# Seven block products in place of eight for a SwiGLU up-projection

## The chip, the cores and the metric

One Trainium2 chip, one of its cores. The metric is the device time of one execution of the whole program in microseconds (us), median of several runs.

## The reference

One decoder layer, sequence 1024, width 1024, all in float32: three token mixers behind one input projection, an output projection, then the feed-forward part, which is what changes here:

```python
def swiglu(h, w_up, w_down):
    gate, val = jnp.split(h @ w_up, 2, axis=-1)
    return (jax.nn.silu(gate) * val) @ w_down
...
        h = rmsnorm(x, norm_ffn[l]) * (1.0 + sc_ffn) + sh_ffn
        x = x + gt_ffn * swiglu(h, w_ffn_up[l], w_ffn_down[l])
    return rmsnorm(x, norm_final)
```

`w_up` is 1024 x 5632 (2816 gate columns, 2816 value columns), `w_down` 2816 x 1024.

## The kernel before

Every float32 matrix is kept as a high part (rounded to the type that TensorE takes, `F32R`) and a low part (the rest), and a product is three matmuls, the `PASSES`: high by high, high by low, low by high. The mixers take the first 1865 us. The change leaves them alone but for a pair of semaphores at the start; what follows is the feed-forward part, `ffn_sp`, `ffn_pool`, `ffn_pe`, `ffn_act` and `ffn_dve`, one function for each engine's queue. The order of the work on an engine is the order in which it is written there; semaphores alone tie the engines together.

The normed activations stand in `h_hi` and `h_lo`, channels on partitions: 8 blocks of 128 channels by 1024 tokens. The loop has 11 steps (`F_STEPS`) of 256 feed-forward columns. In a step TensorE makes eight up-projection units in `UP` (banks 0 to 3), each a column block of 128 by one half of the tokens: 24 matmuls of 512 columns (L180, 8 channel blocks by 3 passes), gate and value in turn. ScalarE takes exp(-gate) from the bank (L2207). VectorE adds 1, takes the reciprocal, multiplies by gate and by value (L2237 to L2241), ScalarE rounds the result to `hid_hi` (L2209), VectorE subtracts for `hid_lo` (L2243). Then TensorE makes 16 down-projection units in `DOWN` (banks 4 to 7), 6 matmuls each (L2191), and VectorE adds each to the residual rows `x1`, in `feat_region` (L2248). The hidden part of a step thus hides behind its later up units, and the 16 adds behind the down units.

SyncE loads raw weights in halves of 512 KB to `w_raw`. GpSimd splits them into high (L161, a cast) and low (L163, a subtraction), into `A_W` for a step's first column block and `B_W` for its second; for `w_down` it first multiplies by the adaLN gates (L2149), then splits to `D_W` (L2150, L2152). GpSimd waits for `up` or `down` before it writes over a buffer. At the end each 128 tokens are normed and stored as their adds are done (`final_norm`).

`D_W` begins at this byte:

```python
    D_W = [over(f"wD_{h}", [P, 2, D], F32R, at_byte["rows_region"] + (4104 + n * 2048) * 4)
           for n, h in enumerate(("hi", "lo"))]
```

In the built program `rows_region`, `h_hi`, `h_lo` and `A_W` begin at multiples of 64 bytes, so `D_W` begins 32 bytes past one; so does `O2_W`, the last weights of the output projection (L1002).

Of the kernel before, what the change touches and what calls it, by code (L numbers as in the profile page):

```python
# [76 lines left out]
def _build(ctx, nc, x, c, ada_w, ada_b, norm_mix, norm_ffn, w_in, gla_w_g2, gla_b_g2, gla_norm,  # L77
# [2045 lines left out]
    def ffn_pool(pool, step):  # L2123
        own = Count(sem("w_split"))
        wait_unit(pool, unit_of("out", NT - 1, 2))
        for j in range(2):
            pool.wait_ge(sem(f"w_in{j}"), 16 * (IN_ALL + 1))
            split(pool, j, A_W, P, own)
        for g in range(GROUPS):
            i, n = divmod(g, 3)  # L2130
            if n == 0:
                if i:
                    pool.wait_ge(sem("up"), 8 * i)
                else:
                    wait_unit(pool, unit_of("out", NT - 1, 3))
            if n == 1:
                if i:
                    pool.wait_ge(sem("down"), 2 * NT * i)
                else:
                    wait_unit(pool, unit_of("o2", NT - 1))  # L2140
                    pool.wait_ge(sem("xt_up"), H0 + 2 * KT)
                    pool.wait_ge(sem("gates_in"), 16)
            if n == 2:
                pool.wait_ge(sem("up"), 8 * i + (4 if i else 6))
            for j in range(2):
                pool.wait_ge(sem(f"w_in{j}"), 16 * (IN_ALL + 2 + g))
                if n == 1:
                    raw = w_raw[:, j].rearrange("p k n -> p (k n)")
                    step(pool.tensor_tensor(raw, raw, gates_ffn, ALU.mult))  # L2149
                    own.inc(pool.tensor_copy(D_W[0][:, j], raw))  # L2150
                    own.wait(pool)
                    own.inc(pool.tensor_tensor(D_W[1][:, j], raw, D_W[0][:, j].bitcast(F32), ALU.subtract))  # L2152
                    own.wait(pool)
# [326 lines left out]
```

## Time and profile before

| | us |
|---|---|
| median of 3 runs (2605.65 to 2610.41) | 2607.14 |
| the profiled execution | 2607.23 |
| its span, first to last instruction | 2605.5 |
| VectorE busy / ScalarE busy / GpSimd busy | 1892.0 / 997.7 / 504.9 |
| TensorE busy | 2543.5 |
| mean granted clock | 0.997 |

1.7 us lie around the span. In a timeline row stand the start, the duration, engine, line, operation, output and inputs; in brackets the idle time before it and what ended it. Durations of TensorE overlap, so the price of a matmul is the distance of the starts.

### The profile page before, as it was taken

Reading aid. Unit: us, or ns where it says so; the run is one execution under the profiler, and the core shown is the slowest. Engines: PE = TensorE matmul, PEld = TensorE weight load, DVE = VectorE, ACT = ScalarE, POOL = GpSimd, SP = SyncE. Lnnn points to the kernel's source line nnn. Section 1 sums busy time; section 2 is a strip of 40 time slices with the busy share of each in tenths; the row PEclk is TensorE's granted clock in tenths of the full one; section 3 lists DMA queues with packets and bytes.
Section 4 is the critical chain, followed back from the end, with each engine's and each line's share of the span. In section 5 each row is a group of like instructions: output and inputs, shape, how many; then the busy total and the mean of one; then the engine's idle time right before and its main releaser. Section 6 shows DMA issues by size and latency. Waiting matters only on the chain.

```text
span 2605.5 us, 44201 instructions
## 1 busy us (share of the span) xinstructions
PE 2543.5 (98%) x16256; PEld 2260.3 (87%) x16256; DVE 1892.0 (73%) x3606; ACT 997.7 (38%) x2220; POOL 504.9 (19%) x440
## 2 busy tenths in 40 slices
PE   6999999999999999999999999999999999999998
PEld 4899889889899989989989989989888888888887
DVE  5688778878878877777777777885666666666666
ACT  6643744654474373364355345333400000000002
POOL 1000401311220130000000000000344444433330
PEclk9999999999999999999999999999999999999999
DMA  7221231132122122223123213241121111111111
GB/s 238 61 65 30 58 80 38 36 94 50 33 70 62 26 57 80 43 50 86 42 48 87 46 33 97 71 135 51 50 65 49 49 45 46 48 49 49 49 41 65
DMA packets 221703, 160.85 MB, mean 62 GB/s; under 512 B 24720, under 2 KB 204024, under 8 KB 221488
## 3 DMA queue, kind: packets, MB, share of 16 engines
q1 hardware_dynamic: 208592, 149.98, 19.8%
q0 software_dynamic: 12896, 8.05, 3.1%
q8 instruction: 130, 2.13, 0.3%
q14 instruction: 85, 0.70, 0.1%
HBM read 141.67 MB, written 16.33 MB: 61 GB/s over the span
## 4 chain that ended last, share of the span: by engine, by line
PE 78%; DVE 14%; ACT 6%; issue 1%; DMA 1%; SPq 0%; DVEq 0%; ACTq 0%
PE bank L180 31%; PE bank L172 21%; PE bank L2191 9%; PE bank L1256 2%; PE bank L1009 2%; PE bank L1262 2%; DVE sig L1089 2%; PE bank L1590 1%; PE bank L1605 1%; PE bank L1213 1%; PE bank L1608 1%; PE bank L1606 1%; DVE feat_region L1702 1%; PE bank L1756 1%; DVE rows_region L1098 1%
## 5 line engine op out<-in xcount | busy, mean ns | idle before, releaser
L172 PE MATMUL bank<-wA_hi,h_hi 128*128 128x256 f32 x1024 | 296.5, 290 | 1.0 <-ACT sig L1061 0.4
L172 PE MATMUL bank<-wB_hi,h_hi 128*128 128x256 f32 x1024 | 296.4, 289 | 0.5 <-ACT sig L1061 0.2
L172 PE MATMUL bank<-wB_lo,h_hi 128*128 128x256 f32 x1024 | 295.5, 289 | 0.0
L172 PE MATMUL bank<-wA_lo,h_hi 128*128 128x256 f32 x1024 | 295.2, 288 | 0.0
L172 PE MATMUL bank<-wB_hi,h_lo 128*128 128x256 f32 x1024 | 295.0, 288 | 0.0
L172 PE MATMUL bank<-wA_hi,h_lo 128*128 128x256 f32 x1024 | 295.0, 288 | 0.0
L180 PE MATMUL bank<-h_hi,wA_hi 128*128 128x512 f32 x672 | 266.0, 396 | 3.1 <-DVE feat_region L1022 1.9
L180 PE MATMUL bank<-h_hi,wB_lo 128*128 128x512 f32 x672 | 265.7, 395 | 0.0
L180 PE MATMUL bank<-h_hi,wA_lo 128*128 128x512 f32 x672 | 265.7, 395 | 0.0
L180 PE MATMUL bank<-h_hi,wB_hi 128*128 128x512 f32 x672 | 265.7, 395 | 0.0
L180 PE MATMUL bank<-h_lo,wA_hi 128*128 128x512 f32 x672 | 265.4, 395 | 0.0
L180 PE MATMUL bank<-h_lo,wB_hi 128*128 128x512 f32 x672 | 265.3, 395 | 0.0
L2312 POOL DMA_DIRECT2D y_scratch<-ybuf x56 | 48.4, 864 | 864.1 <-DVE ybuf L1366 864.1
L172 PEld LDWEIGHTS bank<-wA_hi,h_hi 128*128 128x128 f32 x1024 | 194.6, 190 | 5.0 <-issue 1.7
L172 PEld LDWEIGHTS bank<-wB_hi,h_hi 128*128 128x128 f32 x1024 | 194.6, 190 | 4.2 <-issue 1.8
L172 PEld LDWEIGHTS bank<-wA_hi,h_lo 128*128 128x128 f32 x1024 | 194.7, 190 | 1.0 <-issue 0.7
L172 PEld LDWEIGHTS bank<-wB_hi,h_lo 128*128 128x128 f32 x1024 | 194.7, 190 | 1.1 <-issue 0.7
L172 PEld LDWEIGHTS bank<-wB_lo,h_hi 128*128 128x128 f32 x1024 | 194.6, 190 | 0.8 <-issue 0.7
L172 PEld LDWEIGHTS bank<-wA_lo,h_hi 128*128 128x128 f32 x1024 | 194.6, 190 | 0.8 <-issue 0.7
L1089 DVE RECIPROCAL sig<-sig 128x128 f32<-128x128 f32 x192 | 183.0, 953 | 6.6
L2248 DVE TENSOR_TENSOR feat_region<-feat_region,bank 128x512 f32<-128x512 f32 x176 | 121.1, 688 | 83.2 <-PE bank L2191 80.9
L2207 ACT ACTIVATE conv_in<-bank 128x512 f32<-128x512 f32 x44 | 26.4, 599 | 358.7 <-PE bank L180 358.6
(394 smaller groups left out, 6042.8 us busy)
## 6 DMA issues: line engine op xcount, KB each, us to landing
w_raw<-in_w_in_dram SPq DMA_DIRECT2D x96, 512.0 KB, 4.0
w_raw<-in_w_ffn_up_dram SPq DMA_DIRECT2D x44, 512.0 KB, 3.9
rows_region<-in_ada_w_dram SPq DMA_DIRECT2D x64, 256.0 KB, 2.8
w_raw<-in_w_ffn_down_dram SPq DMA_DIRECT2D x22, 512.0 KB, 3.5
ada<-in_ada_w_dram SPq DMA_DIRECT2D x8, 1024.0 KB, 14.5
conv_in<-row_scratch SPq DMA_DIRECT2D x16, 512.0 KB, 4.5
rows_region<-in_x_dram SPq DMA_DIRECT2D x8, 512.0 KB, 6.8
w_raw<-in_w_in_dram SPq DMA_DIRECT2D x16, 256.0 KB, 2.9
```

The source lines that it names most:

```text
L172: mm = nc.tensor.matmul(bank[:, n_out:n_out + n1 - n0], (h_hi, h_lo)[hp][:, k, t * P:t * P + P], buf[wp][:, k, n0:n1], start=(s == 0), sto ...
L180: mm = nc.tensor.matmul(bank[0:n, :], buf[wp][:, k, n0:n0 + n], (h_hi, h_lo)[hp][:, k, half * HALF:half * HALF + HALF], start=(s == 0), st ...
L1009: mm = nc.tensor.matmul(G[u % 2][:, 0:256], (h_hi, h_lo)[hp][:, k, cols], (A_W, B_W)[g % 2][wp][:, k], start=(s == 0), stop=(s == n_steps( ...
L1089: step(dve.reciprocal(ex, ex), "sig_recip")
L1098: eng.tensor_tensor(factor, base, ex, ALU.mult).then_inc(sem("sig_used"), 1)
L1213: last = mm(M[0][:, c * 256:c * 256 + 256], kq[:, 0, t:t + P], kq[:, :, t:t + P], start=True, stop=True)
L1256: last = mm(M[3][:, c * 64:c * 64 + 64], at[:, c, 0:P], one(xm[:, c], b, 0), start=True, stop=True)
L1262: last = mm(M[3][0:n, 256 + c * 64:320 + c * 64], pm[:, v, c, 0:n], one(xmt[:, c], b, 1), start=True, stop=True)
L2191: mm = nc.tensor.matmul(DOWN[n % 4][:], hid[hp][:, k, t * P:t * P + P], D_W[wp][:, k, half * HALF:half * HALF + HALF], start=(s == 0), sto ...
L2207: step(A(e_buf[:, n % 2], UP[2 * n % 4][:], ACT.Exp, scale=-1.0), "gate_exp")
L2248: step(dve.tensor_tensor(acc, acc, DOWN[n % 4][:], ALU.add), "down_read")
L2312: pool.dma_start(y_dram[t * P:t * P + P, i * P:i * P + P], ybuf[:, t % 2, 0:P], accum_op=ALU.add).then_inc(sem(f"y_add{t % 2}"), 16)
```

## The change

The up-projection now goes by 22 groups of 128 feed-forward columns (`F_GROUPS`) in place of 11 steps of 256. In the first four groups (`PLAIN`) a group is four units of 24 matmuls as before, each of two `product`s of 12 (four channel blocks by three passes). From the fifth on, the product of the weights, as 2 by 2 blocks x11, x12 (gate columns, channels in halves) and x21, x22 (value columns), with the activations, as blocks y11, y12, y21, y22 (channels in halves, tokens in halves), is made from seven block products in Winograd's form, with sums of weights and sums of activations (t1 to t4) as operands. A product is 12 matmuls.

- **GpSimd** (`ffn_pool`) makes in such a group five sums of 128x512 and seven splits (a cast and a subtraction each) into a ring of four `slots`, which lie where `A_W` and `B_W` were, then multiplies the 128x1024 of `w_down` by the gates. The high part of `D_W` is now ScalarE's; the low part, `down_low(g - 1)`, stands between the third and the fourth split of group g.
- **TensorE** (`ffn_pe`): products 1 to 3, then `down(g - 1)`, which is 16 units of 3 matmuls, then products 4 to 7. Partial results are read out of a bank between the products that go on adding to it: product 3 waits for `P1_COPY`, 5 for `U2_COPY`, 6 for `P5_COPY`, 7 for `U3_COPY`.
- **ScalarE** (`ffn_act`) makes these four copies, and the whole sigmoid, as exp(-ln(1 + exp(-x))) in three instructions; VectorE's reciprocal goes.
- **VectorE** (`ffn_dve`) adds up the copies and the banks, multiplies, makes `hid_lo`, and does 16 adds for each group, so 352 in all where there were 176. In groups 2 to 5 it also makes the activation sums: 40 instructions, and 16 for their low parts.
- `hid` and `D_W` have half the size, and `D_W` begins at a multiple of 64 bytes. At the start of the kernel two `ada` loads share a semaphore.

```diff
-    hid = [over(f"hid_{h}", [P, 2, S], F32R, at_byte["rows_region"] + n * 8192) for n, h in enumerate(("hi", "lo"))]
-    D_W = [over(f"wD_{h}", [P, 2, D], F32R, at_byte["rows_region"] + (4104 + n * 2048) * 4)
+    hid = [over(f"hid_{h}", [P, S], F32R, at_byte["rows_region"] + n * 4096) for n, h in enumerate(("hi", "lo"))]
+    D_W = [over(f"wD_{h}", [P, D], F32R, at_byte["rows_region"] + 8192 + n * 4096)
            for n, h in enumerate(("hi", "lo"))]
...
-        sp.dma_start(ada_buf[m][:], ada_v[:, :, o:o + ADA_W]).then_inc(sem(f"ada_in{m}"), 16)
+        sp.dma_start(ada_buf[m][:], ada_v[:, :, o:o + ADA_W]).then_inc(sem(f"ada_in{m // 2}"), 16)
...
-        pe.wait_ge(sem(f"ada_in{m}"), 16)
+        pe.wait_ge(sem(f"ada_in{m // 2}"), 32)
...
+    F_GROUPS = D_FF // P
+    PLAIN, SLOTS, KH = 4, 4, KT // 2
+    slots = [over(f"slot_{n}", [P, 2, KH, P], F32R, at_byte["wA_hi"] + n * 4096) for n in range(SLOTS)]
...
+    def h_place(name, k):
+        return {"y11": (k, 0), "y12": (k, 1), "t1": (k, 1), "y21": (KH + k, 0), "y22": (KH + k, 1)}[name]
...
+        for g in range(F_GROUPS):
+            sp.wait_ge(sem("w_split"), slots_made(g))
+            if g + 1 < F_GROUPS:
+                for j in range(2):
+                    load_half(sp, j, up_cols(g + 1)[j])
+            if g == 0:
                 sp.wait_ge(sem("xt_up"), H0 + 2 * KT)
+                sp.dma_start(d_raw, down_v[:, 0]).then_inc(sem("d_in"), 16)
+            sp.wait_ge(sem("w_split"), d_made(g))
+            if g + 1 < F_GROUPS:
+                sp.dma_start(d_raw, down_v[:, g + 1]).then_inc(sem("d_in"), 16)
...
+        def parts(n, raw):
+            hi, lo = slots[n % SLOTS][:, 0], slots[n % SLOTS][:, 1]
+            do(pool.tensor_copy(hi, raw))
+            do(tt(lo, raw, hi.bitcast(F32), ALU.subtract))
...
+        def down_low(g):
+            pool.wait_ge(sem("taken"), d_high(g))
+            do(tt(D_W[1][:], d_raw, D_W[0][:].bitcast(F32), ALU.subtract))
...
+            x11, x12 = w_raw[:, 0, 0:KH], w_raw[:, 0, KH:KT]
+            x21, x22 = w_raw[:, 1, 0:KH], w_raw[:, 1, KH:KT]
+            pool.wait_ge(sem("w_in0"), 16 * (IN_ALL + 1 + g))
+            slot_free(n)
+            parts(n, x11)
+            slot_free(n + 1)
+            parts(n + 1, x12)
+            pool.wait_ge(sem("w_in1"), 16 * (IN_ALL + 1 + g))
+            if plain(g):
+                if g:
+                    down_low(g - 1)
+                slot_free(n + 2)
+                parts(n + 2, x21)
+                slot_free(n + 3)
+                parts(n + 3, x22)
+            else:
+                slot_free(n + 2)
+                do(tt(raw_of(n + 2, 0), x21, x22, ALU.add))
+                do(tt(raw_of(n + 2, 1), raw_of(n + 2, 0), x11, ALU.subtract))
+                do(tt(x12, x12, raw_of(n + 2, 1), ALU.subtract))
+                parts(n + 2, raw_of(n + 2, 1))
+                down_low(g - 1)
+                slot_free(n + 3)
+                do(tt(raw_of(n + 3, 1), x21, x22, ALU.add))
+                parts(n + 3, raw_of(n + 3, 1))
+                do(tt(x21, x11, x21, ALU.subtract))
+                slot_free(n + 4)
+                parts(n + 4, x21)
+                slot_free(n + 5)
+                parts(n + 5, x12)
+                slot_free(n + 6)
+                parts(n + 6, x22)
+            pool.wait_ge(sem("d_in"), 16 * (g + 1))
+            if g == 0:
+                pool.wait_ge(sem("gates_in"), 16)
+                pool.wait_ge(sem("xt_up"), H0 + 2 * KT)
+            else:
+                pool.wait_ge(sem("down"), 2 * NT * g)
+            do(tt(d_raw, d_raw, gates_ffn, ALU.mult))
...
+        def product(bank, g, n, name, first, last):
+            pe.wait_ge(sem("w_split"), slot_made(g, n))
+            slot = slots[(slot0(g) + n) % SLOTS]
+            for k in range(KH):
+                if g == 0 and name in ("y12", "y22"):
+                    pe.wait_ge(sem("h_lo"), H1 + KT + (0 if name == "y12" else KH) + k + 1)
+                for s, (wp, hp) in enumerate(PASSES):
+                    mm = nc.tensor.matmul(bank[:], slot[:, wp, k], h_block(name, hp, k), start=(first and k == 0 and s == 0),
+                                          stop=(last and k == KH - 1 and s == 2), skip_group_check=True)
...
+        for g in range(PLAIN, F_GROUPS):
+            a = first_bank(g)
+
+            def add(bank, n, name, first, last):
+                product(bank, g, n, name, first, last).then_inc(sem("up"), 1)
+
+            pe.wait_ge(sem("hid_full"), 2 * g - 1 if g == PLAIN else 2 * (g - 1))
+            add(a, 0, "y11", True, False)
+            pe.wait_ge(sem("gate_taken"), 2 * g if g == PLAIN else 2 * g - 1)
+            add(UP[1], 1, "y21", True, True)
+            pe.wait_ge(sem("taken"), took(g, P1_COPY))
+            pe.wait_ge(sem("h_lo"), H_DONE + SUM_AT["t2"] + KH)
+            add(a, 2, "t2", False, False)
+            down(g - 1)
+            pe.wait_ge(sem("gate_taken"), 2 * g)
+            pe.wait_ge(sem("h_lo"), H_DONE + SUM_AT["t1"] + KH)
+            add(UP[2], 3, "t1", True, False)
+            pe.wait_ge(sem("taken"), took(g, U2_COPY))
+            add(a, 4, "t3", False, False)
+            pe.wait_ge(sem("taken"), took(g, P5_COPY))
+            add(UP[2], 5, "y22", False, True)
+            pe.wait_ge(sem("taken"), took(g, U3_COPY))
+            add(a, 6, "t4", False, True)
+        down(F_GROUPS - 1)
...
+        def sigmoid(src):
+            step(A(e_one, src, ACT.Exp, scale=-1.0))
+            step(A(e_one, e_one, ACT.Ln, bias=1.0))
+            step(A(e_one, e_one, ACT.Exp, scale=-1.0), "gate_exp")
...
+        for g in range(PLAIN, F_GROUPS):
+            a = first_bank(g)
+            act.wait_ge(sem("up"), up_done(g, 1))
+            act.wait_ge(sem("hid_lo"), 2 * g)
+            step(A(p1_buf[:], a[:], ACT.Copy), "taken")
+            if g == PLAIN:
+                sum_high("t1", 3)
+            act.wait_ge(sem("up"), up_done(g, 3))
+            step(A(u2_buf[:], a[:], ACT.Copy), "taken")
+            act.wait_ge(sem("gate_taken"), 2 * g + 1)
+            sigmoid(p1_buf[:])
+            act.wait_ge(sem("up"), up_done(g, 4))
+            step(A(p5_buf[:], UP[2][:], ACT.Copy), "taken")
+            act.wait_ge(sem("up"), up_done(g, 5))
+            step(A(u3_buf[:], a[:], ACT.Copy), "taken")
+            down_high(g)
+            act.wait_ge(sem("gate_taken"), 2 * g + 2)
+            sigmoid(u2_buf[:])
+            hid_high(g, 1, 1, u2_buf)
+            hid_high(g, 2, 0, p1_buf)
...
+        def make_t3(k):
+            step(tt(h_tmp("t3", 0, k), h_in("y22", 0, k), h_in("y12", 0, k), ALU.subtract))
+            step(tt(h_tmp("t3", 1, k), h_in("y22", 1, k), h_in("y12", 1, k), ALU.subtract))
+            step(tt(h_tmp("t3", 1, k), h_tmp("t3", 1, k), h_tmp("t3", 0, k), ALU.add), "h_full")
...
+            dve.wait_ge(sem("up"), up_done(g, 2))
+            dve.wait_ge(sem("taken"), took(g, P1_COPY))
+            step(tt(p1_buf[:], p1_buf[:], UP[1][:], ALU.add), "gate_taken")
+            for n in range(2 * NT):
+                down_add(g - 1, n)
+                if g == PLAIN and n == 3:
+                    sum_low("t1", 3)
+            dve.wait_ge(sem("gate_exp"), 2 * g + 1)
+            step(tt(p1_buf[:], p1_buf[:], e_one, ALU.mult))
+            dve.wait_ge(sem("taken"), took(g, U3_COPY))
+            step(tt(u3_buf[:], u3_buf[:], p5_buf[:], ALU.add))
+            dve.wait_ge(sem("up"), up_done(g, 6))
+            step(tt(u2_buf[:], u2_buf[:], UP[2][:], ALU.add), "gate_taken")
+            dve.wait_ge(sem("gate_exp"), 2 * g + 2)
+            step(tt(u2_buf[:], u2_buf[:], e_one, ALU.mult))
+            step(tt(u2_buf[:], u2_buf[:], u3_buf[:], ALU.mult), "hid_full")
+            dve.wait_ge(sem("up"), up_done(g, 7))
+            step(tt(p1_buf[:], p1_buf[:], a[:], ALU.mult), "hid_full")
+            hid_low(g, 1, 1, u2_buf)
+            hid_low(g, 2, 0, p1_buf)
```

GpSimd's queue. The place is the weights' way into one step of the loop before, 256 columns wide:

```order
L161 CAST wA_hi<-w_raw 128x8x128
L163 TENSOR_TENSOR wA_lo<-w_raw,wA_hi 128x8x128
L161 CAST wA_hi<-w_raw 128x8x128
L163 TENSOR_TENSOR wA_lo<-w_raw,wA_hi 128x8x128
L161 CAST wB_hi<-w_raw 128x8x128
L163 TENSOR_TENSOR wB_lo<-w_raw,wB_hi 128x8x128
L161 CAST wB_hi<-w_raw 128x8x128
L163 TENSOR_TENSOR wB_lo<-w_raw,wB_hi 128x8x128
L2149 TENSOR_TENSOR w_raw<-w_raw,conv_in 128x1024
L2150 CAST wD_hi<-w_raw 128x1024
L2152 TENSOR_TENSOR wD_lo<-w_raw,wD_hi 128x1024
```

and one group now, 128 columns wide, from its first two splits over the three sums to `down_low` and on (`slot_raw` is a slot before it is split, `feat_region` here the raw `w_down`):

```order
L2262 TENSOR_TENSOR feat_region<-feat_region,conv_in 128x1024
L2211 CAST slot_68<-w_raw 128x512
L2212 TENSOR_TENSOR slot_68<-w_raw,slot_68 128x512
L2211 CAST slot_65<-w_raw 128x512
L2212 TENSOR_TENSOR slot_65<-w_raw,slot_65 128x512
L2241 TENSOR_TENSOR slot_raw_70<-w_raw 128x512
L2242 TENSOR_TENSOR slot_raw_70<-slot_raw_70,w_raw 128x512
L2243 TENSOR_TENSOR w_raw<-w_raw,slot_raw_70 128x512
L2211 CAST slot_66<-slot_raw_70 128x512
L2212 TENSOR_TENSOR slot_66<-slot_raw_70,slot_66 128x512
L2219 TENSOR_TENSOR wD_lo<-feat_region,wD_hi 128x1024
L2247 TENSOR_TENSOR slot_raw_71<-w_raw 128x512
```

Per 256 columns 14 instructions of 128x1024 have become 42, of which 38 are of 128x512, and `wD_lo` stands behind three sums and a split.

VectorE's queue, at the end of the hidden part. Before:

```order
L2237 TENSOR_SCALAR conv_in<-conv_in 128x512
L2238 RECIPROCAL conv_in<-conv_in 128x512
L2239 TENSOR_TENSOR conv_in<-conv_in,bank 128x512
L2241 TENSOR_TENSOR conv_in<-conv_in,bank 128x512
L2243 TENSOR_TENSOR hid_lo<-conv_in,hid_hi 128x512
L2248 TENSOR_TENSOR feat_region<-feat_region,bank 128x512 x16
L2237 TENSOR_SCALAR conv_in<-conv_in 128x512
```

Now, between the adds of one group and those of the next (`prod` are the four buffers of copies, 123 and 124 those that become the hidden values, `conv_in` the sigmoid):

```order
L2443 TENSOR_TENSOR feat_region<-feat_region,bank 128x512 x16
L2555 TENSOR_TENSOR prod_123<-prod_123,conv_in 128x512
L2557 TENSOR_TENSOR prod_125<-prod_125,prod_126 128x512
L2559 TENSOR_TENSOR prod_124<-prod_124,bank 128x512
L2561 TENSOR_TENSOR prod_124<-prod_124,conv_in 128x512
L2562 TENSOR_TENSOR prod_124<-prod_124,prod_125 128x512
L2564 TENSOR_TENSOR prod_123<-prod_123,bank 128x512
L2448 TENSOR_TENSOR hid_lo<-prod_124,hid_hi 128x512
L2448 TENSOR_TENSOR hid_lo<-prod_123,hid_hi 128x512
L2549 TENSOR_TENSOR prod_123<-prod_123,bank 128x512
```

Six of these instructions have two inputs and both in SBUF (L2555, L2557, L2561, L2562, L2448 twice); before there was one for each hidden tile (L2243).

## Rows read from the trace of the kernel before

**Rows 1.** The page: busy shares of the span; the chain that ended last, by engine.
```profile
PE 2543.5 (98%) x16256; PEld 2260.3 (87%) x16256; DVE 1892.0 (73%) x3606; ACT 997.7 (38%) x2220; POOL 504.9 (19%) x440
...
PE 78%; DVE 14%; ACT 6%; issue 1%; DMA 1%; SPq 0%; DVEq 0%; ACTq 0%
```

**Rows 2.** Windows, one step of the loop: length, busy us (x instructions) by engine, clock, DMA.
```profile
1985.00:2050.90 65.90, 65.90 (x289) 54.00 (x288) 39.32 (x36) 4.92 (x8) 26.12 (x15) 1.00 0.16 49
```

**Rows 3.** Timeline, TensorE: up-projection, down-projection, and an earlier output projection.
```profile
2024.78 0.39 PE L180 MATMUL bank<-h_hi,wB_hi 128*128 128x512 f32 x1
...
2026.82 0.39 PE L180 MATMUL bank<-h_hi,wB_hi 128*128 128x512 f32 x1
...
2574.22 0.40 PE L2191 MATMUL bank<-wD_hi,hid_hi 128*128 128x512 f32 x1
...
2577.96 0.39 PE L2191 MATMUL bank<-wD_hi,hid_lo 128*128 128x512 f32 x1
...
1862.80 0.40 PE L1002 MATMUL bank<-wO_hi,h_hi 128*128 128x512 f32 x1
...
1863.27 0.40 PE L1002 MATMUL bank<-wO_lo,h_hi 128*128 128x512 f32 x1
```

**Rows 4.** Groups by line and shape (count, busy us, mean ns, idle before), from 1900 us on.
```profile
L2248 DVE TENSOR_TENSOR feat_region<-feat_region,bank 128x512 f32<-128x512 f32 x176 | 121.1, 688 | 83.2 <-PE bank L2191 80.9
L2243 DVE TENSOR_TENSOR hid_lo<-conv_in,hid_hi 128x512 fp32r<-128x512 f32 x43 | 65.0, 1511 | 35.6 <-ACT hid_hi L2209 35.6
...
L2209 ACT ACTIVATE hid_hi<-conv_in 128x512 fp32r<-128x512 f32 x43 | 27.2, 632 | 270.9 <-DVE conv_in L2241 270.9
L2207 ACT ACTIVATE conv_in<-bank 128x512 f32<-128x512 f32 x42 | 25.2, 599 | 358.6 <-PE bank L180 358.6
```

**Rows 5.** Groups by line and shape, GpSimd, whole span.
```profile
L1535 POOL TENSOR_TENSOR rows_region<-rows_region 128x512 f32<-128x512 f32 x32 | 41.9, 1310 | 3.1 <-ACT rows_region L1495 0.8 <-POOL rows_region L1535 0.2
```

**Rows 6.** Timeline, GpSimd then VectorE: two low-part subtractions of VectorE.
```profile
1959.11 1.04 POOL L161 CAST wA_hi<-w_raw 128x1024 fp32r<-128x1024 f32 x1 [9.67 <-PE bank L180]
1960.23 2.40 POOL L163 TENSOR_TENSOR wA_lo<-w_raw,wA_hi 128x1024 fp32r<-128x1024 f32 x1
1962.69 1.38 POOL L161 CAST wA_hi<-w_raw 128x1024 fp32r<-128x1024 f32 x1
...
1960.61 2.57 DVE L2243 TENSOR_TENSOR hid_lo<-conv_in,hid_hi 128x512 fp32r<-128x512 f32 x1 [0.83 <-ACT hid_hi L2209]
...
1972.49 0.69 DVE L2243 TENSOR_TENSOR hid_lo<-conv_in,hid_hi 128x512 fp32r<-128x512 f32 x1 [0.83 <-ACT hid_hi L2209]
```

**Rows 7.** Timeline, VectorE then GpSimd: two VectorE instructions, one of GpSimd between.
```profile
281.71 0.88 DVE L1504 TENSOR_TENSOR rows_region<-cum 128x512 f32<-128x512 f32 x1
282.62 1.37 DVE L1702 SCALAR_TENSOR_TENSOR feat_region<-conv_in,conv_w,feat_region 128x1024 f32<-128x1024 f32 x1
...
281.58 0.46 POOL L1527 TENSOR_TENSOR dq<-rows_region,dq 128x128 f32<-128x128 f32 x1 [2.56 <-ACT ke L1490]
282.11 0.80 POOL L1528 TENSOR_TENSOR qd<-rows_region,qd 128x128 f32<-128x128 f32 x1
```

**Rows 8.** Timeline, VectorE: an add behind its matmuls, and the last instructions.
```profile
2578.69 0.69 DVE L2248 TENSOR_TENSOR feat_region<-feat_region,bank 128x512 f32<-128x512 f32 x1 [0.55 <-PE bank L2191]
...
2597.62 3.93 DVE L2222 SCALAR_TENSOR_TENSOR feat_region<-feat_region,gh 128x1024 f32<-128x1024 f32 x3
```

**Rows 9.** Timeline, TensorE: two idle times; windows: the clock after the first.
```profile
1752.01 0.63 PE L1969 MATMUL bank<-ident,feat_region 128*128 128x128 f32 x4 [3.01 <-DVE h_lo L2012]
...
1865.52 0.47 PE L180 MATMUL bank<-h_hi,wA_hi 128*128 128x512 f32 x1 [1.86 <-DVE feat_region L1022]
...
1752.80:1756.20 3.40, 3.25 (x16) 2.95 (x14) 2.06 (x5) 0.53 (x1) 0.00 (x0) 0.50 1.03 411
```

**Rows 10.** DMA issues (KB, us to landing), and the matmuls on the last pair.
```profile
ada<-in_ada_w_dram SPq DMA_DIRECT2D x8, 1024.0 KB, 14.5
...
42.30 2.14 PE L459 MATMUL bank<-ada,c_act 128*32 128x256 f32 x32
```

More of the change, by code:

```diff
@@ new lines, in _build @@
+    sums = {name: [[over(f"h{name}_{p}_{k}", [P, HALF], F32R, HOLES[8 * n + 4 * p + k]) for k in range(KH)]
+                   for p in range(2)] for n, name in enumerate(("t2", "t3", "t4"))}
+    sums_raw = {name: [[over(f"raw{name}_{p}_{k}", [P, HALF], F32, HOLES[8 * n + 4 * p + k]) for k in range(KH)]
+                       for p in range(2)] for n, name in enumerate(("t2", "t3", "t4"))}
+    p1_buf, u2_buf, u3_buf, p5_buf = (over(f"prod_{n}", [P, HALF], F32, HOLES[24 + n]) for n in range(4))
@@ L2124, in ffn_pool @@
         own = Count(sem("w_split"))
-        wait_unit(pool, unit_of("out", NT - 1, 2))
[L2126 to L2153, printed above, removed]
-                else:
-                    split(pool, j, (B_W, None, A_W)[n], P, own)
@@ new lines, in ffn_pool, with plain_unit, down @@
+        down_low(F_GROUPS - 1)
+    def ffn_pe(pe):
+        def product(bank, g, n, name, first, last):
[7 more added lines that the diff above has]
+                                          stop=(last and k == KH - 1 and s == 2), skip_group_check=True)
+            return mm
+        def plain_unit(bank, g, gv, half):
+            product(bank, g, 2 * gv, ("y11", "y12")[half], True, False)
+            product(bank, g, 2 * gv + 1, ("y21", "y22")[half], False, True).then_inc(sem("up"), 1)
+        def down(g):
+            pe.wait_ge(sem("w_split"), d_made(g))
+            pe.wait_ge(sem("hid_lo"), 2 * g + 2)
@@ L2183, in ffn_pe @@
             for n in range(2 * NT):
                 t, half = n // 2, n % 2
-                if n % NT == 0:
-                    pe.wait_ge(sem("hid_lo"), 4 * i + 3 + n // NT)
-                if 2 * NT * i + n >= 4:
-                    pe.wait_ge(sem("down_read"), 2 * NT * i + n - 3)
-                for s in range(6):
-                    k, (wp, hp) = s // 3, PASSES[s % 3]
-                    mm = nc.tensor.matmul(DOWN[n % 4][:], hid[hp][:, k, t * P:t * P + P],
-                                          D_W[wp][:, k, half * HALF:half * HALF + HALF], start=(s == 0),
-                                          stop=(s == 5))
@@ L2194, in ffn_pe @@
-                mm.then_inc(sem("down"), 1)
+                if 2 * NT * g + n >= 4:
+                    pe.wait_ge(sem("down_read"), 2 * NT * g + n - 3)
+                for s, (wp, hp) in enumerate(PASSES):
+                    mm = nc.tensor.matmul(DOWN[n % 4][:], hid[hp][:, t * P:t * P + P],
+                                          D_W[wp][:, half * HALF:half * HALF + HALF], start=(s == 0), stop=(s == 2))
+                mm.then_inc(sem("down"), 1)
+        for u in range(2):
+            pe.wait_ge(sem(f"proj_read{u}"), (N_UNITS - u + 1) // 2)
@@ L2200, in ffn_act @@
             nrm_hi(act, step, n)
[L2201 to L2209 removed]
+        act.wait_ge(sem("up"), up_done(0, 1))
@@ L2251, in ffn_dve @@
+        for n in range(2 * NT):
+            down_add(F_GROUPS - 1, n)
+            if n % 2 and n >= 5:
+                final_norm(n // 2 - 2)
         final_norm(NT - 2)
```

295 lines of the change are left out of this document (222 added, 73 removed).

## The prediction

> **What bounds the kernel now.** I read the page first. TensorE is busy for 98% of the span and carries 78% of the chain that ended last; VectorE has 73% [rows 1]. These shares are means over two stages that have nothing in common, so the feed-forward loop is read from its own windows. In one step TensorE has no idle time at full clock, VectorE works 39.3 of 65.9 us and GpSimd 26.1 [rows 2]. The loop is bound by TensorE, and only fewer or cheaper matmuls, or new stalls of TensorE, can move it. The price of a matmul is the distance of starts: nine L180 distances take 2.04 us, so 0.2267 each; sixteen L2191 distances take 3.74 us, so 0.2337 [rows 3]. A step is 192 x 0.2267 + 96 x 0.2337 = 65.96 us, as its window says.
>
> **Fewer matmuls.** The up-projection has 11 x 192 = 2112 matmuls before, and 4 x 96 + 18 x 84 = 1896 after: 216 x 0.2267 = **-49.0 us**. The down-projection keeps its 1056.
>
> **Cheaper matmuls.** The down-projection's matmuls have the same 512 columns and the same type as L180's, and cost 7 ns more. What they share with L1002, whose distances are 0.235 [rows 3], is streamed weights that begin 32 bytes past a multiple of 64; L180 streams from multiples of 64. After the change `D_W` begins on such a multiple, so I take 0.2267 for it: 1056 x 0.0070 = **-7.4 us**. The bounds are 0 and -7.4. The Trainium skill (SBUF — State Buffer, Door 1: The DMA port swizzle) tells of 16-byte lines as what an access pays for; by it both addresses are as good and the sum would be 7.4 us higher. The rows differ by the address and I go by them.
>
> **The pair of GpSimd and VectorE.** This is what decides. A `hid_lo` subtraction (two inputs, both in SBUF) takes 0.69 us alone, but 2.57 when it begins 0.38 us into a GpSimd subtraction: it ends 0.55 us after GpSimd's, and GpSimd's next cast takes 1.38 in place of 1.04 [rows 6]. So one of the two runs at a time, for a whole instruction, and a waiting one starts 0.14 us before the other's end. When VectorE has a second one at once, GpSimd gets in between: L1528, 0.46 alone (as L1527), takes 0.80 and ends after the first VectorE instruction but long before the second [rows 7]. They alternate. An add from a bank, L2248, stays at 0.688 in the mean with and without GpSimd beside it [rows 4], so it is free of this. Before, GpSimd works 40% of a step and the hidden part has four such subtractions, all with slack. After, GpSimd works some 80% of a group, and without a gap where VectorE's chain runs.
>
> Prices of the new instructions: VectorE 0.69 for 128x512; ScalarE 0.60 and 0.63 [rows 4]; 0.03 between instructions of either. GpSimd's subtraction of 128x512: between half of 2.40, which is 1.20 [rows 6], and the mean of L1535, 1.31 [rows 5], whose mean holds some blocked ones; I take 1.27. Its cast: half of 1.04 and some start-up, 0.57 (0.52 to 0.65). 0.07 lies between its instructions [rows 6]. VectorE starts 0.50 after the last matmul of a unit starts [rows 3, 8], so 0.27 after TensorE is free.
>
> One group from the sixth on, with 0 at the start of product 7 (product 6 has just ended). VectorE adds the bank to `u2_buf`, 0.27 to 0.96; ScalarE's three instructions, 1.05 to 3.00. GpSimd, freed by product 6, makes its three sums, 0.27 to 4.23. VectorE wants L2561 at 3.09, gets in at 4.09 and ends at 4.78. GpSimd's cast ends at 5.21. VectorE's L2562 ends at 5.76, GpSimd's low part at 6.89. L2564 reads a bank and runs to 6.48. The first `hid_lo` is ready at 6.57 and ends at 7.44. GpSimd has asked in the meantime for `down_low`, 2.40 long, and ends at 9.70; the second `hid_lo` ends at 10.25. ScalarE may only now copy into `p1_buf`: 10.94, and TensorE starts product 3 at 10.99. It had work (products 7, 1, 2) for 8.16: **idle 2.83**. From there product 3, 48 down matmuls and products 4 to 6 take 96 x 0.2267 = 21.76, so a group is 32.75 us. Without the blocking the chain ends at about 7.5 and a group is its 132 matmuls, 29.92. The wait arises 17 times: **+48 us**. The step before was 32.98 for the same 128 columns: the saving is nearly eaten. GpSimd's own work, 12 x 1.27 + 7 x 0.57 + 2 x 2.40 + 21 x 0.07 = 25.5 us, fits; loads of 3.5 to 5 us have more than that of time. These cost nothing.
>
> **Groups 2 to 5.** Here the activation sums fall into VectorE's queue ahead of the adds. Between the adds of the first and second down part there are 26 instructions, 26 x 0.72 = 18.8 us, in 32.6 - 11.6 = 21.0, and 22 of them alternate with GpSimd's ten; followed like the group above, the adds come 4.5 us late and TensorE waits for its banks. The 20 instructions of the last such stretch do the same, +4.5. GpSimd's splits, slowed likewise, come late for product or unit by 3.4 and 2.4. In between 17 instructions fit. **+15 us**, less the 0.5 that TensorE waits there today; between 5 (VectorE's count alone) and 20.
>
> **The end.** Before, from the first down matmul of the last step, 2574.22, to VectorE's last instruction, 2597.62 + 3.93 = 2601.55, are 27.3 us [rows 3, 8]. After, from the end of the last product: 4.1 for the hidden part (nothing to hide behind), 0.95 to the first add, 16 x 0.72 + 6 x 1.32 of norms between and 2.6 for the last two: 27.1. No change. But the matmuls ahead of this point count: 21 x 48 x 0.2267 in place of 10 x 96 x 0.2337, so the -7.4 becomes **+4.2** up to here, and the rest of it lies in the last down part, where VectorE is slower anyway. At the start the seventh `ada` block waits for the eighth's load (14.5 us to landing, used in the stretch of 42.30 [rows 10]): **+0.7**.
>
> **The clock.** The granted clock fell to 0.50 over 1752.8 to 1756.2 after TensorE had sat idle for 3.01 us, and did not after 1.86 [rows 9]. That fall cost half of its 3.4 us, 1.7. Idle times of 2.83 lie between; I take two falls in 17, **+3.4** (0 to 17 x 1.7 = 29).
>
> Sum: -49.0 + 4.2 + 48.1 + 14.6 + 0.7 + 3.4 = **+22 us** on an execution of 2607.23 with a span of 2605.5; the median of the runs is 2607.14, the same. The forecast is **2629 us**. About 0.2%, 5 us, is what can be told from no change.
>
> **Rivals.**
> 1. *The two engines don't queue up in the hidden part* (faster). If the second `hid_lo` slips in ahead of `down_low` and the rest is short, the chain ends under 8.1 and the 48 us and the falls of the clock go: 2629 - 51 = 2578. For it: GpSimd has 7 us to spare in a group, and a queue that runs a little later or earlier than worked out here would leave gaps where VectorE asks; against: the alternation in [rows 6, 7], which leaves GpSimd always next while it has work. It decides when 2.8 us of the blocking are saved. Chance 0.13.
> 2. *`hid_lo` meets a short GpSimd instruction in place of the 2.40 one*: 1.13 less, 17 times, -19: 2608, no change. It hangs on 0.4 us of drift between the queues. Chance 0.06.
> 3. *The address isn't why down matmuls cost more*: 0.0070 x 1008 = +7: 2636. Chance 0.11.
> 4. *The clock falls in every group*: +29 - 3 : 2655. For it: 2.83 is near 3.01. The Trainium skill (TensorE: Matmul & The Clock Gate, HAM oscillation) has idle time between bursts bring back the lower clock burst after burst; by it this rival would be the rule. No run here shows it at 2.83. Chance 0.06.
> 5. *The order or the matmul count isn't what I read*: the order shows 84 + 48 matmuls per group and 216 fewer in all, so none.
>
> **The numbers.** The forecast has 0.64, rivals 3 and 4 add 0.17 on the slower side: slower 0.81, faster 0.14 (rival 1 and a part of what surrounds 2), within 0.2% 0.05. The forecast's own bounds are -12 (GpSimd at 1.20, groups 2 to 5 at +5) and +12 (1.31 and 0.65, four more falls). The range, 2604 to 2648, takes in rivals 2 and 3 and leaves out 1 and 4.
>
> **What would show it.** L2448 at two durations, the later one 2.5 us and more beside the GpSimd subtraction `wD_lo`; TensorE idle some 2.8 us before each product 3, ended by ScalarE's copy; groups 32.7 apart; down matmuls 0.227 apart; waits of 4 us for adds in the second and fourth down part. Wrong: L2448 near 0.69 to 1.3, groups 29.9 apart, a span near 2575.

## The result, and the profile after

| | us |
|---|---|
| after, median of 4 runs (2666.15 to 2669.86) | 2667.07 |
| before, beside it (4 runs, 2605.65 to 2610.41) | 2608.19 |
| ratio | 1.0228, 95% interval 1.021 to 1.0246 |
| span of the profiled execution after | 2664.7 |
| forecast | 2629 (2604 to 2648) |

The change makes the kernel 59 us slower, 38 us more than the forecast and outside its range. The page answers to [rows 1]: 216 matmuls fewer, yet TensorE's share fell from 98 to 95% of a longer span, and VectorE's part of the chain rose from 14 to 20%.

```profile
PE 2533.1 (95%) x16040; PEld 2244.0 (84%) x16040; DVE 1962.5 (74%) x3804; ACT 1130.7 (42%) x2418; POOL 750.8 (28%) x704
...
PE 69%; DVE 20%; ACT 8%; issue 2%; DMA 1%; POOL 0%; SPq 0%; ACTq 0%; DVEq 0%; POOLq 0%
```

TensorE's waits from 1860 us on (total, times, longest). Before there were three waits here, of 1.9, 0.9 and 0.5 us. Now the first line is the forecast's idle time ahead of product 3, and the others are its waits for adds, for splits (the last of them, 2.6, stands ahead of the very first product, where the 1.9 stood before) and, as "issue", for the last low halves of `hid`.

```profile
PE bank L2274 <- ACT prod L2407: 46.6, 17, 2.7
PE bank L2290 <- DVE feat_region L2443: 9.8, 5, 4.0
PE bank L2274 <- POOL slot L2212: 5.3, 2, 3.4
PE bank L2290 <- issue: 3.9, 1, 3.9
PE bank L2274 <- POOL slot L2211: 2.6, 1, 2.6
```

The chain of one group, in order of time (start, us, what). Counted from the start of product 7, 2284.92, VectorE's add starts at 0.26 and L2561 at 3.11, the second `hid_lo` ends at 10.40, ScalarE's copy at 11.12, and product 3 starts at 11.16; the forecast had 0.27, 3.09, 10.25, 10.94 and 10.99.

```profile
2279.86 5.23 PE bank L2274 x23
2285.14 0.04 issue
2285.18 0.70 DVE prod L2559
2285.92 0.04 issue
2285.97 0.64 ACT conv_in L2344
2286.63 0.64 ACT conv_in L2345
2287.30 0.64 ACT conv_in L2346
2288.03 1.80 DVE prod L2561
2289.86 0.99 DVE prod L2562
2290.95 0.65 ACT hid_hi L2352
2291.69 0.87 DVE hid_lo L2448
2292.58 2.74 DVE hid_lo L2448
2295.43 0.61 ACT prod L2407
2296.08 3.03 PE bank L2274 x12
```

GpSimd beside it (start, us, engine, line, operation). The second `hid_lo`, 0.69 alone [rows 6], asks at 2292.58, 0.51 after `wD_lo` has begun, and ends 0.56 after it.

```profile
2290.38 1.62 POOL L2212 TENSOR_TENSOR slot<-slot_raw,slot 128x512 fp32r<-128x512 f32 x1
2292.07 2.69 POOL L2219 TENSOR_TENSOR wD_lo<-feat_region,wD_hi 128x1024 fp32r<-128x1024 f32 x1
2294.84 1.60 POOL L2247 TENSOR_TENSOR slot_raw<-w_raw 128x512 f32<-128x512 f32 x1
```

So far all is as forecast. What is not stands in TensorE's own rows: product 3 in two groups, both behind an idle time of 2.74 us, is 4.51 us long in the one and 3.03 in the other.

```profile
2087.25 4.51 PE L2274 MATMUL bank<-ht,slot 128*128 128x512 f32 x12 [2.74 <-ACT prod L2407]
...
2296.08 3.03 PE L2274 MATMUL bank<-ht,slot 128*128 128x512 f32 x12 [2.74 <-ACT prod L2407]
```

The windows of these two groups, and of 3.4 us behind the first of the two idle times (length, busy us by engine, granted clock, DMA):

```profile
2073.00:2107.60 34.60, 31.86 (x134) 25.85 (x133) 21.78 (x25) 8.52 (x13) 26.47 (x22) 0.95 0.16 46
2087.10:2090.50 3.40, 3.25 (x8) 2.61 (x9) 0.69 (x1) 0.09 (x1) 3.18 (x4) 0.50 0.41 142
2280.00:2314.40 34.40, 31.66 (x140) 25.79 (x139) 21.81 (x26) 8.85 (x14) 27.70 (x23) 1.00 0.15 47
```

The granted clock was 0.50, the lower of the two levels, in the second of them. Read by the distance of GpSimd's L2262 starts, groups without a fall are 33.07 us apart, with one 34.3 to 34.7, with a longer one 35.9 and 36.0; 14 of the 17 distances are of the last two kinds. The forecast had two in 17.

The down matmuls start 0.2266 us apart (47 distances from 2298.95 to 2309.60), in place of 0.2337 [rows 3].

```profile
2298.95 0.39 PE L2290 MATMUL bank<-wD_hi,hid_hi 128*128 128x512 f32 x1
...
2309.60 0.39 PE L2290 MATMUL bank<-wD_lo,hid_hi 128*128 128x512 f32 x1
```

### The profile page after: what moved, and what is told of

It is laid out like the page before. It is cut to its first block, busy times and chain, and to the rows that moved or that the text cites. A ratio compares the mean times of both kernels' runs of the same rounds, so it can differ in the third digit from the quotient of the medians.

```text
span 2664.7 us, 45007 instructions
## 1 busy us (share of the span) xinstructions
PE 2533.1 (95%) x16040; PEld 2244.0 (84%) x16040; DVE 1962.5 (74%) x3804; ACT 1130.7 (42%) x2418; POOL 750.8 (28%) x704
## 4 chain that ended last, share of the span: by engine, by line
PE 69%; DVE 20%; ACT 8%; issue 2%; DMA 1%; POOL 0%; SPq 0%; ACTq 0%; DVEq 0%; POOLq 0%
PE bank L172 21%; PE bank L180 13%; PE bank L2274 10%; PE bank L2290 9%; DVE hid_lo L2448 2%; PE bank L1254 2%; PE bank L1007 2%; PE bank L1260 2%; DVE sig L1087 2%; PE bank L1588 1%; DVE prod L2561 1%; PE bank L1603 1%; PE bank L1211 1%; PE bank L1606 1%; PE bank L1604 1%
## 5 line engine op out<-in xcount | busy, mean ns | idle before, releaser
L2443 DVE TENSOR_TENSOR feat_region<-feat_region,bank 128x512 f32<-128x512 f32 x352 | 242.0, 687 | 91.2 <-PE bank L2290 79.7
L2274 PE MATMUL bank<-h_hi,slot 128*128 128x512 f32 x832 | 268.2, 392 | 6.0 <-POOL slot L2212 3.4
L2274 PE MATMUL bank<-ht,slot 128*128 128x512 f32 x648 | 184.0, 439 | 48.5 <-ACT prod L2407 46.6
L2274 PEld LDWEIGHTS bank<-ht,slot 128*128 128x128 f32 x648 | 137.2, 215 | 87.8 <-ACT prod L2407 56.0
L2274 PEld LDWEIGHTS bank<-h_hi,slot 128*128 128x128 f32 x832 | 157.0, 189 | 41.1 <-issue 4.5
L2274 PE MATMUL bank<-h_lo,slot 128*128 128x512 f32 x416 | 162.8, 391 | 0.0
L2290 PE MATMUL bank<-wD_hi,hid_hi 128*128 128x512 f32 x352 | 141.0, 400 | 13.7 <-DVE feat_region L2443 9.8
L2212 POOL TENSOR_TENSOR slot<-w_raw,slot 128x512 fp32r<-128x512 f32 x106 | 148.8, 1404 | 8.5
```

What stands on the lines that cost most here:

```text
L2212: do(tt(lo, raw, hi.bitcast(F32), ALU.subtract))
L2274: mm = nc.tensor.matmul(bank[:], slot[:, wp, k], h_block(name, hp, k), start=(first and k == 0 and s == 0), stop=(last and k == KH - 1 and ...
L2290: mm = nc.tensor.matmul(DOWN[n % 4][:], hid[hp][:, t * P:t * P + P], D_W[wp][:, half * HALF:half * HALF + HALF], start=(s == 0), stop=(s = ...
L2443: step(tt(acc, acc, DOWN[n % 4][:], ALU.add), "down_read")
```

## The experiments

Two questions: is all of the idle time the chain of GpSimd and VectorE, and is the clock's fall its consequence? Beside these, the other main terms of the sum were tried by themselves. Each run is compared with the kernel before, run beside it on the same chip; not all of the runs shared one chip.

| run | median us | before beside it | ratio, 95% interval |
|---|---|---|---|
| after + 12 matmuls in the idle time | 2642.00 | 2607.88 | 1.0109 to 1.0139 |
| after + 6 matmuls | 2641.48 | 2608.16 | 1.0114 to 1.0142 |
| after + 3 matmuls | 2655.77 | 2610.70 | 1.0161 to 1.0192 |
| GpSimd holds back `down_low` | 2606.21 | 2607.88 | 0.9982 to 1.0001 |
| `down_low` in two halves | 2620.86 | 2610.70 | 1.0028 to 1.0061 |
| buffers change places | 2588.51 | 2607.88 | 0.9904 to 0.9937 |
| the same, five plain groups | 2587.09 | 2608.16 | 0.9907 to 0.9934 |
| all groups plain | 2616.24 | 2608.16 | 1.0022 to 1.0046 |
| before, loads of `ada_w` in pairs | 2608.72 | 2607.88 | 0.9993 to 1.0011 |
| before, `D_W` on a multiple of 64 | 2600.91 | 2608.16 | 0.9963 to 0.9982 |

### The idle time filled with work

```diff
             add(UP[1], 1, "y21", True, True)
+            pe.wait_ge(sem("down_read"), 2 * NT * (g - 1))
+            for _ in range(12):
+                nc.tensor.matmul(DOWN[0][:], h_hi[:, 0, 0:P], h_hi[:, 0, 0:HALF], start=True, stop=True)
             pe.wait_ge(sem("taken"), took(g, P1_COPY))
```

> The changed kernel with 12 extra matmuls of 512 columns (2.72 us of TensorE, result thrown away) in every group from the fifth on, just ahead of the wait before product 3: TensorE computes through its idle time and nothing else changes. Theory A (the idle of 2.7 us in each group is what brings the granted clock down, and that costs 1.6 us a group more): the clock stays at 1 in the 18 groups, each group lasts 33.1 instead of 34.6 us, and the time falls by some 25 us, from 2667 to 2642 us. Rival B (the clock falls for another reason, such as the load of the new groups as a whole): it falls as often as before, 2667 us. Rival C (more activity makes the clock fall more): over 2675 us.

Measured: 2642.00, 25.1 us less than after, by adding 216 matmuls. No group of the 17 has a fall; all are 33.1 us apart. The clock's price in these groups is about that 25 us, and it comes of the idle time: the only other change is a wait for VectorE's reads of the bank that the extra matmuls write, which no row shows to cost anything. Theory A; B and C are out.

How much idle time does it take here? The same with 6 and with 3 matmuls:

> As the run with 12 extra matmuls a group, with 6 (1.36 us), so that 1.4 us of the idle time before product 3 stay. Groups last 33.1 us if the clock stays at 1, 34.6 if it falls. Theory A1 (the clock falls for an idle stretch of this size too): as the changed kernel, 2665 us. Theory A2 (1.4 us are too little to bring it down; the kernel with the wait on GpSimd had 0.9 us and kept its clock): 2642 us, as with 12.

> As the runs with 12 and with 6 extra matmuls a group, with 3 (0.68 us), so that 2.06 us of the idle time stay; the clock kept up with 1.4 us left and fell in 14 of 17 groups with 2.74. If it keeps up: 2642 us. If it falls as often as in the changed kernel: 2665 us; between, if it falls in a part of the groups.

Measured: 2641.48 with 6 and 2655.77 with 3. TensorE's waits, first with 6, then with 3:

```profile
PE bank L2274 <- ACT prod L2410: 24.1, 17, 1.4
```

```profile
PE bank L2274 <- ACT prod L2410: 35.5, 17, 2.1
```

With 1.4 us left no group distance is over 33.2; with 2.1 left 10 of 17 are 34.7, and the time lies between the two expectations. So this stop costs nothing beyond itself at 1.4 us (nor at 0.7, in the run with a wait on GpSimd below), 1.6 us more in 10 of 17 cases at 2.1, and in 14 of 17 at 2.74.

### GpSimd holds back its long subtraction

```diff
                 parts(n + 2, raw_of(n + 2, 1))
+                pool.wait_ge(sem("hid_lo"), 2 * g)
                 down_low(g - 1)
```

> The changed kernel with one wait added: GpSimd's subtraction that makes the low half of the down weights (2.67 us each) waits until VectorE has made the low half of hid of the group before. Theory A (GpSimd and VectorE take turns, and this one long instruction between VectorE's two lengthens the chain to ScalarE's copy of product 1): the second low half of hid ends 2 us earlier, idle before product 3 shrinks from 2.8 to about 0.7 us a group, the clock no longer falls there, and the time is 2667 - 17 x 2.1 - 25 = 2600 to 2610 us. Rival B (taking turns is not the cause; the chain is as long without it): GpSimd waits and nothing is gained, 2665 to 2680 us.

Measured: 2606.21. The wait for ScalarE's copy is 0.7 a group in place of 2.74, and with it every fall of the clock in the 17 groups is gone.

```profile
PE bank L2275 <- ACT prod L2408: 11.9, 17, 0.7
```

VectorE's low halves of `hid` between 2060 and 2560 us took 691, 772 and 865 ns (least, median, most); after, 850, 1793 and 2733. One wait added to an engine with slack takes 61 us from the time.

### The same subtraction in two halves

```diff
-            do(tt(D_W[1][:], d_raw, D_W[0][:].bitcast(F32), ALU.subtract))
+            for c in (slice(0, HALF), slice(HALF, D)):
+                do(tt(D_W[1][:, c], d_raw[:, c], D_W[0][:, c].bitcast(F32), ALU.subtract))
```

(The counts of `w_split` are raised to match.)

> The changed kernel with GpSimd's subtraction for the low half of the down weights (128x1024, 2.67 us) made as two of 128x512; its place in GpSimd's order stays, nobody waits for anything new. Theory A (the two engines take turns by whole instructions; followed with the durations of the trace, VectorE's second low half of hid waits for 1.3 us of GpSimd in place of 2.4): it ends 1.1 us earlier, the idle time before product 3 is 1.6 to 1.7 us in place of 2.74, L2448 falls from a mean of 1.73 to 1.2 us, and the clock, which stayed up with 1.4 us of idle time, stays up here too: 2667 - 19 - 25 = 2620 to 2626 us; 2645 us if it falls with 1.7 us. Rival B (the two share a port and slow each other evenly, whatever the size of an instruction): no change of the idle time, 2665 us.

Measured: 2620.86, in the range of theory A with the clock up. Timeline, VectorE, GpSimd, ScalarE:

```profile
2267.76 2.55 DVE L2449 TENSOR_TENSOR hid_lo<-prod,hid_hi 128x512 fp32r<-128x512 f32 x2
...
2268.15 3.28 POOL L2220 TENSOR_TENSOR wD_lo<-feat_region,wD_hi 128x512 fp32r<-128x512 f32 x2
...
2270.42 0.60 ACT L2408 ACTIVATE prod<-bank 128x512 f32<-128x512 f32 x1 [2.05 <-DVE hid_lo L2449]
```

```profile
PE bank L2275 <- ACT prod L2408: 28.6, 17, 1.7
```

VectorE's pair takes 2.55 in place of 3.63, since the second now gets in between the two halves. The mean of VectorE's low halves of `hid` from 2050 us on falls from 1.73 to 1.22 us, with 1.2 expected. The wait goes from 2.74 to 1.7 and no group has a fall: 32.00 apart, all 17. Even slowing would not care how the work is cut, so rival B is out. The Trainium skill (SBUF — State Buffer, Who interferes with whom) calls the ports that the two share an exclusive lock, held for the whole instruction; these rows agree.

### The buffer that ends the chain

```diff
+    SWAP = ((p1_buf, p5_buf), (p5_buf, p1_buf))
...
         for g in range(PLAIN, F_GROUPS):
             a = first_bank(g)
+            p1_buf, p5_buf = SWAP[g % 2]
             act.wait_ge(sem("up"), up_done(g, 1))
-            act.wait_ge(sem("hid_lo"), 2 * g)
+            if g == PLAIN:
+                act.wait_ge(sem("hid_lo"), 2 * g)
             step(A(p1_buf[:], a[:], ACT.Copy), "taken")
+            act.wait_ge(sem("hid_lo"), 2 * g)
             act.wait_ge(sem("up"), up_done(g, 3))
```

(VectorE's loop takes the same pair.)

> The changed kernel with product 1 copied into the buffer that product 5 had in the group before (the two change places each group), so ScalarE's copy no longer waits for the low half of hid. Everything else, GpSimd's order too, stays. Theory A (all of the idle time before product 3 comes down this one chain, and the half clock with it): no idle time before product 3, groups of 29.9 to 30.5 us instead of 34.6, and 2667 - 47 - 25 = 2595 us, down to 2585 us if waits that stand behind it leave too. Rival B (another wait stands right behind: the down part's for hid, or GpSimd's slots, by 2 us a group or more): 2630 us or more.

Measured: 2588.51, the first version that beats the kernel before, by 0.8%. GpSimd's order is untouched, and `hid_lo` is as slow as ever (up to 2782 ns); it has merely left TensorE's path. TensorE's waits from 1860 us on, and windows of the early groups and of one with seven products:

```profile
PE bank L2291 <- DVE feat_region L2449: 9.8, 5, 4.0
PE bank L2275 <- POOL slot L2213: 5.3, 2, 3.4
PE bank L2291 <- issue: 3.9, 1, 3.9
PE bank L2275 <- POOL slot L2212: 2.6, 1, 2.6
```

```profile
1900.00:1935.00 35.00, 33.15 (x139) 27.28 (x140) 32.41 (x36) 7.80 (x12) 15.48 (x12) 0.95 0.16 47
1935.00:1970.00 35.00, 31.05 (x129) 24.73 (x128) 32.38 (x42) 9.86 (x15) 11.39 (x9) 0.95 0.15 44
...
2005.00:2035.00 30.00, 24.66 (x94) 19.28 (x93) 27.18 (x28) 5.60 (x9) 23.02 (x18) 0.89 0.18 53
```

```profile
2073.00:2103.04 30.04, 30.04 (x133) 24.77 (x133) 21.82 (x26) 8.53 (x13) 26.44 (x22) 1.00 0.19 53
```

A group is 30.04 us without a wait, 0.12 above its 132 matmuls. From 33.1 to 30.04 in 17 groups is 52 us, and the runs with the idle time filled stand 53.5 us above this one: that is the chain's price without the clock. What is left above the matmuls lies in the first groups: VectorE is busy 32.4 of 35 us, TensorE waits and the clock falls four times there and once in the last down part.

### More room for the sums of activations

The swap (the first group with seven products now copies product 1 without waiting for `hid_lo` too), with `PLAIN = 5`, and the makes and low parts of the sums spread over groups 1 to 5 by a table (group: places ahead of the gate, ahead of `take_up`, behind the adds, behind `hid_low`, behind the second gate; M makes, L is the low part):

```diff
-    PLAIN, SLOTS, KH = 4, 4, KT // 2
+    PLAIN, SLOTS, KH = 5, 4, KT // 2
...
+    WHEN = {
+        1: ('M3.0', 'M3.1', 'M3.2', 'M3.3', 'M2.0 M2.1'),
+        2: ('M2.2 L3.0', 'L3.1', 'M2.3', 'L3.2 L3.3 M4.0', 'M4.1'),
+        3: ('M4.2', 'L2.0', 'M4.3', 'L2.1 L2.2 L2.3', 'L4.0 L4.1'),
+        4: ('L4.2 L4.3', '', 'M1.0 M1.1', 'M1.2', 'M1.3 L1.0'),
+        5: ('L1.1 L1.2', 'L1.3')}
```

> The kernel with the two buffers that change places (2588.5 us), with five plain groups ahead of those with seven products in place of four, and the sums of activations spread over them: in groups 2 to 5 VectorE was busy 31 to 32 of every 35 us, and TensorE waited 7.4 us in two stalls for its adds, at half clock behind each. Theory (VectorE's overload by the sums makes those stalls): one more plain group +2.7 us, stalls down to 1 to 3 us in place of 7.4, two falls of the clock fewer (-3), and 2 to 5 us for a wait on ScalarE's copy in the first group with seven products: 2583 to 2590 us. Rival (the stalls are not VectorE's load): 2591 us or more.

Measured: 2587.09, as expected, though its interval overlaps the four-group version's, so the two can't be told apart. The long waits for adds are gone, as the theory has it, and the clock stayed up from 1900 to 2035 us, though TensorE stood still for 3.4 us from 1902.8 on, a stop that brought it down in the swapped kernel:

```profile
PE bank L2285 <- ACT prod L2407: 4.4, 1, 4.4
PE bank L2301 <- issue: 3.9, 1, 3.9
PE bank L2285 <- POOL slot L2223: 3.4, 1, 3.4
PE bank L2301 <- DVE feat_region L2445: 2.9, 4, 1.1
```

```profile
1900.00:1935.00 35.00, 31.59 (x140) 25.86 (x139) 31.16 (x35) 8.68 (x13) 16.28 (x11) 1.00 0.16 45
```

One more plain group, a wait on ScalarE in the first group with seven products and the clock's fall behind it took back what they gave.

### The new structure without the seven products

`PLAIN = F_GROUPS`, and every make, high and low part of the sums of activations left out: all 22 groups have eight products.

> The changed kernel with all 22 groups made as its first four (eight products), the sums of activations left out: the new groups of 128 columns, ScalarE's sigmoid and the pipelined down part alone. Theory of the forecast (the new structure costs only its first waits for GpSimd's parts, 3.4 us, and for the last low halves of hid, 4.1; the aligned down weights give 7.4 back): 2608 + 7.5 - 7.4 + 3 to 5 for the clock = 2610 to 2616 us, groups of 32.7 us. Rival (the structure itself costs, by turns of GpSimd and VectorE in every group): 2630 us or more.

Measured: 2616.24, just above the range. By the starts of L2262 the groups are 32.64 us apart, which is 144 x 0.2267, and a window in them is full of matmuls at clock 1.00. So the structure costs nothing per group.

```profile
2100.00:2132.70 32.70, 32.70 (x146) 27.09 (x145) 16.15 (x22) 6.06 (x9) 12.77 (x11) 1.00 0.17 49
```

The seven products, with the waits that their sums of activations bring, are worth the 28 us between this run and the swapped one, and in the kernel after they cost 51.

### Two terms alone, in the kernel before

```diff
-        sp.dma_start(ada_buf[m][:], ada_v[:, :, o:o + ADA_W]).then_inc(sem(f"ada_in{m}"), 16)
+        sp.dma_start(ada_buf[m][:], ada_v[:, :, o:o + ADA_W]).then_inc(sem(f"ada_in{m // 2}"), 16)
...
-        pe.wait_ge(sem(f"ada_in{m}"), 16)
+        pe.wait_ge(sem(f"ada_in{m // 2}"), 32)
```

> The kernel before with one part of the change alone: two loads of ada_w share a semaphore, and TensorE waits for both of a pair. Forecast on record: +0.7 us. What the trace of after suggests (the feed-forward part begins 3.9 us later there, half of it by a clock that falls while TensorE waits for the pair): +3 to +4 us, 2611 to 2612 us against 2608. If it is less than 1.5 us, the 3.9 us came from something else in the change.

Measured: +0.84 us, interval -1.8 to +2.9. The forecast's +0.7 lies in it, and so does nothing at all; +3 to +4 is out, so the 3.9 us were mostly something else. Of them 0.7 is the first product's wait for GpSimd's split, 2.58 us where before 1.86 passed; every run made from the changed kernel has it. In the swapped kernel the part begins only 0.5 us later than before, but the clock did not fall at 1753 and 1770 us there, as it did in the traces of before and after. The rest of the 3.9 stays open.

```diff
-    D_W = [over(f"wD_{h}", [P, 2, D], F32R, at_byte["rows_region"] + (4104 + n * 2048) * 4)
+    D_W = [over(f"wD_{h}", [P, 2, D], F32R, at_byte["rows_region"] + 16384 + n * 8192)
```

> The kernel before with the down weights' two tiles moved from 32 bytes past a multiple of 64 bytes to a multiple of 64, and nothing else. Theory of the forecast (the address is why 1,056 down matmuls start 0.2337 us apart and the others 0.2267): 0.2267 in the trace, and 7.4 us less, 2608 to 2600.5 us. Rival (it is the operands' pairing or the order of the six passes): 0.2337 and 2608 us.

Measured: 7.25 us less. The down matmuls start 0.2267 us apart (15 distances in the rows below):

```profile
2568.54 0.39 PE L2191 MATMUL bank<-wD_hi,hid_hi 128*128 128x512 f32 x1
...
2571.94 0.39 PE L2191 MATMUL bank<-wD_hi,hid_hi 128*128 128x512 f32 x1
```

Nothing but the start address was changed, so it is the cause, and rival 3 is out. This one-line version, at 2600.91, beats the kernel before too.

## Why the prediction was wrong

| step | forecast | measured | by |
|---|---|---|---|
| fewer matmuls | -49.0 | 216 fewer | the page |
| cheaper down matmuls, up to the end point | +4.2 (-7.4 in all) | -7.25 in all | `D_W` moved in the kernel before |
| the pair, 17 groups | +48.1 | 46.6 of waits; +52 to 53.5 of time | waits; filled against swapped |
| groups 2 to 5 | +14.6 | 4.0 + 3.4 of waits for adds, 3.4 + 1.9 for splits, less 0.5 before: 12.2 | waits, to 2030 us |
| the first product | 0 | 2.6 in place of 1.9: +0.7 | waits |
| the end | 0 (4.1 for the hidden part) | 3.9 for the hidden part | "issue" wait |
| loads in pairs | +0.7 | +0.8 | alone in the kernel before |
| the clock | +3.4 | +25 in the 17 groups, +9.4 elsewhere | filled run; 18.8 us of work at half rate (17.1 and 8.5 in the swapped kernel) |

With the measured values, each good to about 1 us, the sum is -49.0 + 4.2 + 53 + 12.2 + 0.7 + 0.8 + 25 + 9.4 = +56.3, against 58.9 measured. Most of the 2.6 that is missing lies ahead of this part: the first product's wait begins 3.2 us later than before, and the pairs explain 0.8 of them. With 2.0 (17 x 0.12) in place of the chain's 53, and 8.5 for the clock, it is -20.6, against -19.4 for the swapped kernel.

**The step that failed** is "I take two falls in 17, +3.4". The mechanism, its place and its price per fall were right (1.7; measured 1.3 to 1.6, and 2.8 to 2.9 for the two longer ones, 1.7 in the mean); the number was 14. Its own rows said so: a fall at 3.01, none at 1.86 [rows 9], and 2.83 is nearest to the first. The rule of the nearest row would have made rival 4 the forecast, at 2655. And the trace of the kernel before has a row that [rows 9] leave out, about 100 us ahead of the stop of 1.86: a fall behind 1.90 us, with TensorE less busy around it than in the loop (the second line is a window, its clock 0.50).

```profile
1768.93 0.35 PE L1009 MATMUL bank<-wA_hi,h_hi 128*128 128x256 f32 x1 [1.90 <-DVE h_lo L2012]
...
1769.90:1773.20 3.30, 3.30 (x17) 3.30 (x17) 0.82 (x4) 0.76 (x1) 0.00 (x0) 0.50 0.00 0
```

So 1.86 was no safe bound: in the kernel before with loads in pairs that very stop of 1.86 us has a fall behind it (0.50 from 1866.0 us on). Read with these rows, falls in most of the groups were the forecast to make at 2.83. The Trainium skill (TensorE: Matmul & The Clock Gate, HAM oscillation) has idle time between bursts bring back the lower clock burst after burst, in an example with waits of about 3 to 5 us; the trace agrees, and shows it for a shorter one, 2.74 us, in 14 groups of 17. The example's waits are longer than 2.83, so that section by itself did not make rival 4 the rule, as the prediction puts it; the rows did.

The same step forgot the sum's own stalls in groups 2 to 5 and in the last down part: it forecast five waits of 2.4 to 4.5 us and gave none of them a fall. All five came, of 1.9 to 4.0 us, each with a fall behind it, 9.4 us in all. Together the clock took 34 us in place of 3.4, which is 31 of the 38 us by which the forecast was off.

**The pair of engines** was right in its order, its place and nearly its size: the second `hid_lo` beside `wD_lo`, ScalarE's copy behind it, 2.74 us of waiting for 2.83. It cost 53 us where 48 were forecast: the chain's end is 0.17 later than worked out, and a group without waits 0.12 longer, 17 times each.

**The rivals.** Rival 1, the engines not queueing up, is in effect the run that holds back `down_low`, where `hid_lo` has 772 ns. Rival 2's shorter blocking didn't come by itself; cut in halves it is 1.06 us less waiting a group, near the 1.13 that the rival had (its 2608 should read 2610, 2629 - 19). Rival 3 fell with `D_W` moved. Rival 4 is what happened, though in 14 groups of 17, and with more behind it than its 29 us, since it too counted only the 17 groups.

## What to carry to other kernels

A recurring stop of TensorE has two prices, its length and the half clock behind it; when a forecast finds one, list every stop of the trace with and without a fall behind it, and take the falls from the nearest rows for each stop, the early and the last ones too. When a long GpSimd instruction with SBUF inputs may start just ahead of a two-input VectorE instruction on the critical chain, first ask what makes the chain critical: here a buffer written too early, and one exchange of two buffers was worth 79 us, more than reordering or cutting the instruction (61 and 46). And look at where streamed operands begin: here 32 bytes were worth 7 us.
